# The first stage of a hybrid decoder block: odd k tiles multiplied in plain fp32, even ones still split in two

## The reference, cut to what matters

```python
mod = silu_c @ w_ada[l] + b_ada[l]
sh1, sc1, g1, sh2, sc2, g2 = jnp.split(mod, 6, axis=-1)
h = modulate(rms_norm(x, norm1_w[l]), sh1, sc1)   # rms_norm(x) * (1 + sc1) + sh1
proj = h @ w_in[l]
...                                               # 8 retention heads, 8 differential-attention heads
x = x + g1[:, None, :] * mixed
h2 = modulate(rms_norm(x, norm2_w[l]), sh2, sc2)
x = x + g2[:, None, :] * (jnp.square(jax.nn.relu(h2 @ w_mlp1[l])) @ w_mlp2[l])
return rms_norm(x, final_norm_w)
```

## Time and profile before

| | |
|---|---|
| runs of the kernel before | 2503.66 us median of 3 (2500.78 to 2506.98) |
| the profiled execution, its own time | 2503.31 us |
| its span | 2501.5 us |
| TensorE matmul busy | 2390.8 us (96%) |
| VectorE busy | 1284.5 us (51%) |
| ScalarE busy | 754.9 us (30%) |
| rounding w_hi L579, 400 of them | 422.6 us, 1057 ns each |
| rest w_lo L821, 400 of them | 502.8 us, 1259 ns each |
| mean granted TensorE clock | 0.98 |

### The profile page before, as it was taken

The page is one execution under the profiler, slowest core; times in us unless marked ns, Lnnn a source line. Parts: engine busy times, 40 slices in busy tenths (PEclk is TensorE's granted clock), DMA queues, the critical chain, the costliest instruction groups (busy, mean ns, idle before and its releaser), DMA issues.

```text
span 2501.5 us, 28435 instructions
## 1 busy us (share of the span) xinstructions
PE 2390.8 (96%) x10412; PEld 1936.7 (77%) x10412; DVE 1284.5 (51%) x1680; ACT 754.9 (30%) x1014; POOL 185.0 (7%) x121
## 2 busy tenths in 40 slices
PE   4889999999999999899999999999999999999996
PEld 3667778877777778788888888888888888888885
DVE  7979999885565643453333333333333333333354
ACT  3233234334434532242222221221221221222232
POOL 0003323222212110000000000000000000000000
PEclk9899999999999999899999999999999999999998
DMA  9857877842122332222222222222222222222222
GB/s 361 337 195 269 284 261 254 280 168 76 68 75 67 110 107 95 76 93 101 92 92 101 92 92 98 95 92 95 96 95 92 96 96 92 95 98 92 94 91 84
DMA packets 98309, 328.24 MB, mean 131 GB/s; under 512 B 10064, under 2 KB 18768, under 8 KB 98128
## 3 DMA queue, kind: packets, MB, share of 16 engines
q1 hardware_dynamic: 97248, 326.41, 37.6%
q10 hardware_dynamic: 1008, 1.13, 0.2%
HBM read 323.31 MB, written 4.19 MB: 131 GB/s over the span
## 4 chain that ended last, share of the span: by engine, by line
issue 58%; PE 32%; DVE 6%; ACT 2%; DMA 1%; POOL 0%; DVEq 0%; SPq 0%; POOLq 0%; ACTq 0%
PE bank L359 9%; PE bank L360 9%; PE bank L363 9%; DVE ada_sb L828 3%; PE bank L458 1%; DVE w_lo L821 1%; ACT w_hi L579 1%; PE bank L396 1%; DMA raw<-weights 1%; PE bank L398 0%; PE bank L397 0%; DVE ssq L879 0%; DMA xy<-x_t 0%; PE bank L424 0%; PE bank L402 0%
## 5 line engine op out<-in xcount | busy, mean ns | idle before, releaser
L359 PE MATMUL bank<-act_hi,w_hi 128*128 128x512 f32 x2176 | 871.6, 401 | 40.4 <-DVE act_lo L872 33.5
L360 PE MATMUL bank<-act_lo,w_hi 128*128 128x512 f32 x2176 | 864.3, 397 | 0.0
L579 ACT ACTIVATE w_hi<-raw 128x1024 fp32r<-128x1024 f32 x400 | 422.6, 1057 | 1009.3 <-PE bank L363 1005.0
L821 DVE TENSOR_TENSOR w_lo<-raw,w_hi 128x1024 fp32r<-128x1024 f32 x400 | 502.8, 1259 | 414.0 <-ACT w_hi L579 400.8
L363 PE MATMUL bank<-act_hi,w_lo 128*128 128x512 f32 x2176 | 538.3, 389 | 0.0
L359 PEld LDWEIGHTS bank<-act_hi,w_hi 128*128 128x128 f32 x2176 | 419.9, 193 | 136.0 <-issue 45.0
L360 PEld LDWEIGHTS bank<-act_lo,w_hi 128*128 128x128 f32 x2176 | 419.5, 193 | 87.4
L363 PEld LDWEIGHTS bank<-act_hi,w_lo 128*128 128x128 f32 x2176 | 408.9, 188 | 85.2
L359 PE MATMUL bank<-u_hi,w_hi 128*128 128x512 f32 x1024 | 407.0, 397 | 0.0
L360 PE MATMUL bank<-u_lo,w_hi 128*128 128x512 f32 x1024 | 405.9, 396 | 0.0
L1177 DVE SCALAR_TENSOR_TENSOR xy<-bank,modr,xy 128x512 f32 (+1 forms) x144 | 108.1, 751 | 457.1 <-PE bank L363 457.1
(11 more groups left out here) (127 smaller groups left out, 1208.5 us busy)
## 6 DMA issues: line engine op xcount, KB each, us to landing
raw<-weights SPq DMA_DIRECT2D x400, 512.0 KB, 3.2
ada_sb<-ada SPq DMA_DIRECT2D x172, 512.0 KB, 5.0
prob<-ada SPq DMA_DIRECT2D x20, 512.0 KB, 6.7
xy<-x_t SPq DMA_DIRECT2D x16, 512.0 KB, 6.1
out<-xy SPq DMA_DIRECT2D x4, 1024.0 KB, 9.1
decay_sb<-decay SPq DMA_DIRECT2D x7, 256.0 KB, 4.1
silu_c<-c_row SPq DMA_DIRECT2D x1, 1024.0 KB, 5.5
rot_sb<-rot ACTq DMA_DIRECT2D x2, 256.0 KB, 7.0
```

Of the source, the lines that this page charges most:

```text
L359: pe.matmul(acc[:], stationary, hi, start=first, stop=False)
L360: pe.matmul(acc[:], stationary, lo, start=False, stop=False)
L579: nc.scalar.activation(w_hi[:, w], raw[:, r], ACT.Copy).then_inc(hi_ready, 1)
L821: nc.vector.tensor_tensor(w_lo[:, w], raw[:, r], w_hi[:, w].bitcast(F32), ALU.subtract).then_inc(lo_ready, 1)
```

## The change

Chunks of odd k tiles of the first stage (WHOLE) are not split. ScalarE writes h itself, hf plus shift, in fp32 over `xy[:, k]`, whose x has been read by then (`modulated_hi`), in addition to act_hi, which the later stages need; VectorE still makes act_lo. TensorE then multiplies the landed fp32 chunk in `raw` by that tile, in one plain fp32 matmul for each block (`whole_chunk`). The ring w_hi and w_lo holds split chunks alone (`w_place`, `w_before`), and ScalarE rounds the even chunk of the next group after the modulated_hi of a group. A raw place of an odd chunk is free when TensorE has done with it.

```diff
@@ -77,6 +77,10 @@
 GROUP_OF = {k: g for g, ks in enumerate(K_GROUPS) for k in ks}


+WHOLE = tuple(range(1, KT, 2))
+SPLIT = tuple(k for k in range(KT) if k not in WHOLE)
+
+
 Y_SPLITS = ((2, 3, 4), (5, 6, 7), (8, 9), (10, 11, 12), (13, 14), (), (15,))


@@ -121,6 +125,27 @@
     if not a.above(A_RET):
         return a.base % NADA_1, a.base // NADA_1 + 1
     return a.place(NADA), a.value(NADA, 1 + -(-A_RET // NADA_1) - A_RET // NADA)
+
+
+def made(s):
+
+    if s.above(FIRST):
+        return s.value(1, 1 - len(WHOLE))
+    return SPLIT.index(s.base) + 1
+
+
+def w_place(s):
+
+    return (s + (KT - len(WHOLE))).place(NW) if s.above(FIRST) else SPLIT.index(s.base) % NW
+
+
+def w_before(s):
+
+    if s.terms:
+        return s.value(1, 1 - NW)
+    chunks = SPLIT + tuple(range(FIRST, s.base + 1))
+    i = chunks.index(s.base) - NW
+    return chunks[i] + 1 if i >= 0 else None


 def block_kernel(nc, x_t, c, ada, weights, vecs, lams, rot, decay, ident_in, mask_in, out):
@@ -249,7 +274,7 @@
         sq_ready, ssq_ready = sem("sq_ready"), sem("ssq_ready")
         mean_done, tok_v_ready, tok_r_ready = sem("mean_done"), sem("tok_v_ready"), sem("tok_r_ready")
         diag_ready, spread_done, r_all_ready = sem("diag_ready"), sem("spread_done"), sem("r_all_ready")
-        hf_ready = sem("hf_ready")
+        hf_ready, h_ready = sem("hf_ready"), sem("h_ready")
         act_hi_ready, act_ready = sem("act_hi_ready"), sem("act_ready")
         q_read, k_read, q_ready, k_ready = sem("q_read"), sem("k_read"), sem("q_ready"), sem("k_ready")
         v_ready, gate_ready, y_ret_ready = sem("v_ready"), sem("gate_ready"), sem("y_ret_ready")
@@ -281,8 +306,11 @@
         def _(sp):
             def load_raw(s):
                 r = s.place(NRAW)
-                if s.above(NRAW):
-                    sp.wait_ge(lo_ready, s.value(1, 1 - NRAW))
+                before = s + -NRAW
+                if not s.terms and before.base in WHOLE:
+                    sp.wait_ge(chunk_done, before.base + 1)
+                elif s.above(NRAW):
+                    sp.wait_ge(lo_ready, made(before))
                 sp.dma_start(raw[:, r], weights[s.value()]).then_inc(raw_landed[r], 16)

             def load_ada(a):
@@ -350,15 +378,15 @@
             def split_products(pairs, s):


-                w = s.place(NW)
-                pe.wait_ge(hi_ready, s.value(1, 1))
+                w = w_place(s)
+                pe.wait_ge(hi_ready, made(s))
                 for i, acc, hi, lo, first, _, ready in pairs:
                     if ready is not None:
                         pe.wait_ge(*ready)
                     stationary = w_hi[:, w, i * P128:(i + 1) * P128]
                     pe.matmul(acc[:], stationary, hi, start=first, stop=False)
                     pe.matmul(acc[:], stationary, lo, start=False, stop=False)
-                pe.wait_ge(lo_ready, s.value(1, 1))
+                pe.wait_ge(lo_ready, made(s))
                 for i, acc, hi, _, _, last, _ in pairs:
                     mm = pe.matmul(acc[:], w_lo[:, w, i * P128:(i + 1) * P128], hi, start=False, stop=last)
                 mm.then_inc(chunk_done, 1)
@@ -373,6 +401,15 @@

                 split_products([(i, bank[i], act_hi[:, k], act_lo[:, k], k == 0, k == KT - 1,
                                  (act_ready, k + 1) if i == 0 else None) for i in range(BLOCKS)], Count(k))
+
+            def whole_chunk(k):
+
+                pe.wait_ge(raw_landed[k % NRAW], 16 * (k // NRAW + 1))
+                pe.wait_ge(h_ready, WHOLE.index(k) + 1)
+                for i in range(BLOCKS):
+                    mm = pe.matmul(bank[i][:], raw[:, k % NRAW, i * P128:(i + 1) * P128], xy[:, k],
+                                   start=k == 0, stop=k == KT - 1)
+                mm.then_inc(chunk_done, 1)

             def quad_chunk(s, j, ready0):

@@ -489,7 +526,10 @@
             token_scale(1)
             pe.wait_ge(r_all_ready, 1)
             for k in range(KT):
-                first_chunk(k)
+                if k in WHOLE:
+                    whole_chunk(k)
+                else:
+                    first_chunk(k)
             pe.wait_ge(setup_ready, 2)
             for h in range(1, EARLY + 1):
                 project(h, Count(FIRST + 6 * (h - 1)), 6, ret_stage)
@@ -572,10 +612,11 @@
         @block.scalar
         def _(act):
             def round_w(s):
-                r, w = s.place(NRAW), s.place(NW)
+                r, w = s.place(NRAW), w_place(s)
                 act.wait_ge(raw_landed[r], 16 * s.value(NRAW, 1))
-                if s.above(NW):
-                    act.wait_ge(chunk_done, s.value(1, 1 - NW))
+                before = w_before(s)
+                if before is not None:
+                    act.wait_ge(chunk_done, before)
                 nc.scalar.activation(w_hi[:, w], raw[:, r], ACT.Copy).then_inc(hi_ready, 1)

             def spread(n):
@@ -586,6 +627,8 @@

                 act.wait_ge(hf_ready, KT * n + k + 1)
                 shift = mod1[:, k, 1:2] if n == 0 else modr[:, 1, k:k + 1]
+                if n == 0 and k in WHOLE:
+                    nc.scalar.activation(xy[:, k], hf[:, k % 2], ACT.Identity, bias=shift).then_inc(h_ready, 1)
                 nc.scalar.activation(act_hi[:, k], hf[:, k % 2], ACT.Identity, bias=shift).then_inc(act_hi_ready, 1)

             def square_x(m, x_wait):
@@ -700,18 +743,19 @@
             act.dma_start(rot_sb[:, 0], rot[0, 0]).then_inc(rot_landed, 16)
             act.dma_start(rot_sb[:, 1], rot[0, 1]).then_inc(rot_landed, 16)
             act.dma_start(decay_sb[:], decay[0]).then_inc(decay_landed, 16)
-            round_w(Count(0))
+            if 0 in SPLIT:
+                round_w(Count(0))
             spread(1)
-            round_w(Count(1))
             for g, ks in enumerate(K_GROUPS):
                 for k in ks:
                     modulated_hi(0, k)
-                for k in ks:
-                    if k + 2 <= FIRST:
-                        round_w(Count(k + 2))
+                for k in K_GROUPS[g + 1] if g + 1 < len(K_GROUPS) else ():
+                    if k in SPLIT:
+                        round_w(Count(k))
                 if g == 5:
                     act.wait_ge(lam_dotted, 1)
                     nc.scalar.activation(lam_exp[:], lam_sum[:], ACT.Exp).then_inc(lam_exped, 1)
+            round_w(Count(FIRST))
             round_rotated(1, q_hi)
             for h in range(2):
                 take_gate(h, bank[3 + h], Count(FIRST))
@@ -816,8 +860,8 @@
         @block.vector
         def _(dve):
             def rest_w(s):
-                r, w = s.place(NRAW), s.place(NW)
-                dve.wait_ge(hi_ready, s.value(1, 1))
+                r, w = s.place(NRAW), w_place(s)
+                dve.wait_ge(hi_ready, made(s))
                 nc.vector.tensor_tensor(w_lo[:, w], raw[:, r], w_hi[:, w].bitcast(F32), ALU.subtract).then_inc(lo_ready, 1)

             def dot_ada(a, to):
@@ -1098,7 +1142,8 @@
                 for k in ks:
                     modulated_rest(0, k)
                 for k in ks:
-                    rest_w(Count(k))
+                    if k in SPLIT:
+                        rest_w(Count(k))
                 for k, e in dots[2:]:
                     dots1(k, e)
                 if dots:
```

## The result

The changed kernel takes 2487.69 us (median of 4 runs, 2486.24 to 2490.45), the kernel before 2505.32 us (4 runs beside them). The ratio is 0.9932, 95% interval 0.9915 to 0.9948. In a second set of runs the ratio was 0.9937 (0.9924 to 0.9951), 2489.01 against 2502.73 us. The profiled execution took 2490.45 us with a span of 2488.7, where the one of before took 2503.31 and 2501.5. Of all runs in this document one, of the kernel with half of the plain work left out, took 3969.18 us at a mean granted clock of 0.558; it stays out of that kernel's figures, and its cause is open.

What follows compares the result with a forecast made beforehand. A loop through TensorE, ScalarE and VectorE was taken to bound the first stage. Removing 5.77 us of waits and the rests gave 16.6 us, less 0.6 for clock: 16 us, hence 2487.7 us, range 2482 to 2495.

Steps and rivals of the forecast that it cites:

- the 16 of the sum: First stage: chunk 15 ends at 146.7 instead of 163.35, 16.6 us gained, less 0.6 for a lower-clock stretch.
- VectorE's pair: First stage: without 0.27 us of waiting and one 1.14 us rest, VectorE's 15.16 us per pair becomes 13.75.
- Hf of tile 15 at 135.4: End of first stage on VectorE: 5.77 us of waits and 7.98 of rests go, moving it from 149.49.
- The loop through the rounding: First stage: act_hi stood behind ScalarE's late w_hi rounding; cutting this removes 5.77 us of VectorE's waits.
- The plain matmul: TensorE, odd chunks: 0.853 us per 512-column fp32 matmul, so a plain chunk takes 6.83 us against 5.43 split.
- the upper bound of 9.5: Rival, plain matmul at 1.18 us: chunk 9.5, pair 14.9, 4.7 us gained; 0.08 shared with part given back.
- The eleven microseconds lie in idle time: First stage: TensorE's 8 x 1.4 = 11 us extra fits, needing 12.26 us a pair against VectorE's 13.75.
- The clock's 0.6 us: End of first stage: a lower-clock stretch costs up to 1.8 us, only one near the end survives; 0.6 taken off.
- The 1.77 us that the prediction put on each pair before: Kernel before, TensorE: each pair loses this to the 1.2 GHz level that follows idle time.
- The loads: Rival: ten transfers take 13.0 to 14.0 us a pair; at 14.0, 2489.5 us; 0.2 shared with clock in every pair.
- All that follows waits for chunk 15's end and moves with it: After the first stage: later work keeps the whole 16 us, giving 2487.3 us profiled and 2487.7 on the median.

Runs made afterwards that it cites:

- the time given back: Changed kernel with an idle VectorE subtraction of the same size in place of each dropped rest: 2494.75 us, ratio to the kernel before 0.9960.

## Why the prediction was right, point by point

The time of 2487.7 us was measured to the tenth, and that is luck. The stage gained about a microsecond more than the 16 of the sum, the heads gave 4.4 back, and the rest of the agreement is the spread of the runs: the two sets put the gain at 17.6 and 13.7 us, the two profiled executions at 12.9. The mechanism of the stage is what was right.

- **VectorE's pair**, 13.75 us worked out, 13.66 measured. Hf of tile 15 at 135.4 worked out, 134.1 measured, of which 0.6 is that hf of tile 0 was earlier in this execution (30.47, before 31.08). The step is shown by the time given back: 7 x 1.14 = 8.0 expected, 5.8 to 7.1 measured in the runs, 8.45 at hf of tile 15 in the traces.
- **The loop through the rounding** (5.77 us of waits and the lower clock): shown from both sides. Cutting it alone gave 8.0 us. Closing it again in the changed kernel left 3.7 of the stage's 17.2 us, and of the whole kernel's gain nothing clear of noise.
- **The plain matmul**, 0.853 us: its records are those of the earlier trace rows (610 ns in the mean, one slow chunk with them). A chunk took 7.03 us from its first start to its last end, and its starts are 6.87 us from the next chunk's where chunks follow each other. 6.83 was right, and the upper bound of 9.5 out of reach. An estimate from the Trainium skill's spacing ("TensorE: Matmul & The Clock Gate", section "Back-to-back issue gap"), four times 216 ns for each of eight matmuls, gives 6.9 us and agrees with these rows as well; for the split chunk the same spacing gives 5.18 us, and the measured 0.226 us a matmul decides for 5.43.
- **"The eleven microseconds lie in idle time"** holds for the pairs: taking half of the plain work out gave nothing there. It does not hold for chunks 13 and 15, which lie on the path at the end. The sum did count both at 6.83 us, so the time was not hurt; with half of their work gone the rotation came 6.8 us earlier, and with chunk 15 split again 1.6.
- **The clock's 0.6 us** for a late stretch: mis-sized, it was nothing. After chunk 1 all plain chunks ran at the higher level. The 1.77 us that the prediction put on each pair before went in six of the seven: behind the 2.70 us ahead of pair (13, 14), at 143.79, the granted clock stayed at 1.00.
- **The loads**: the rival was priced at 13.0 to 14.0 us a pair; they carry one in 13.66 without VectorE waiting. How far below that they could go is open: with all chunks plain one pair took 12.78 us and the next ones 13.55 to 14.30, but there the queue waited for TensorE too.
- **"All that follows waits for chunk 15's end and moves with it"** is the step that failed. The stage gained 17.2 us and not 16.6, and 4.8 were lost in the first three heads by a lower granted clock, of which about half a microsecond came back, so 12.8 by the profiles (12.9 by the profiled executions' own times). The medians of the two sets say 13.7 and 17.6. The forecast of 16 lies between them. Why the clock of the heads depends on what stands ahead of them stays open.

## What to carry to other kernels

A small operation queued behind one that waits for the slowest engine's last work closes a loop through all engines; look at the order on that engine before changing the work, since here the order alone brought 8 us where the whole change brought 14 to 18. A dearer product on an engine can be free when that engine is idle for longer than the extra time and nothing else waits for its end; with the loop closed, the same product brought 3.7 us in the stage and nothing clear of noise in the whole kernel. When a bound falls, the next may stand close behind it: work out every engine's and the loads' time for a pair, not their busy shares.

## What the runs showed of the hardware that was not expected

- The first two full heads had the same work and idle times within 0.13 us of each other, and were granted 0.92 of the clock in the changed kernel and 0.96 before, in two profiles each; with the stretch ahead of them (0.72 against 1.00) this cost 4.8 us. Idle times of 3.49 to 6.01 us in place of 2.24 behind chunk 15 brought the first stretch back to 1.00, and 4.75 the next head to 0.96 as well. The kernel with the order alone changed shows 0.92 in both heads without a plain matmul. What decides it stays open.
- After idle times of 1.91 us, the plain chunks behind them ran at the higher level in some pairs (7.11 us) and at the lower in part in others (8.80 us), within one execution. In the changed kernel, after 0.73 to 1.31 us, none did. In the kernel before, the lower level followed the waits of 2.69 to 4.93 us ahead of the first six pairs, but neither the 2.70 us ahead of the last pair nor the 2.69 us ahead of chunk 15.
- The sixteen DMA engines show a share of 0.99 to 1.01 at 370 to 393 GB/s in the changed kernel's pairs without VectorE waiting once; the share said 0.93 at 352 before. A full share alone did not mean a wait.
